# Delta rule of a two-model transformer kernel: the chunk inverse on four 64x64 tiles, with its transpose accumulated on the other half of the partitions

## The reference

```python
    decay = jnp.exp(jnp.where(causal, gcum[..., :, None] - gcum[..., None, :], -jnp.inf))
    kb = kc * bc[..., None]
    m = jnp.where(strict, jnp.einsum('nbhid,nbhjd->nbhij', kb, kc) * decay, 0.0)
    eye = jnp.eye(CHUNK, dtype=f32)
    t_inv = lax.linalg.triangular_solve(eye + m, jnp.broadcast_to(eye, m.shape), left_side=True, lower=True)
    u = t_inv @ (vc * bc[..., None])
    w = t_inv @ (kb * jnp.exp(gcum)[..., None])
    qk = jnp.einsum('nbhid,nbhjd->nbhij', qc, kc) * decay
```

## Time and profile before

| | us |
|---|---|
| median of three runs | 2900.84 |
| the profiled execution, its own time | 2904.52 |
| its span in the profile | 2902.7 |
| TensorE busy, matmuls | 2799.6 (96%) |
| VectorE busy | 2083.9 (72%) |
| ScalarE busy | 1454.1 (50%) |

### The profile page before, as it was taken

How to read it: one execution, slowest core, us unless ns; L and a number is a source line. 1 busy time by engine, 2 the same in 40 slices (tenths; PEclk the granted TensorE clock), 3 DMA queues, 4 the chain that set the end, 5 groups by cost and what they waited for, 6 DMA issues and landing times. The chain is left out here.

```text
span 2902.7 us, 53557 instructions
## 1 busy us (share of the span) xinstructions
PE 2799.6 (96%) x22724; PEld 2498.5 (86%) x22724; DVE 2083.9 (72%) x3259; ACT 1454.1 (50%) x1957; POOL 154.4 (5%) x257
## 2 busy tenths in 40 slices
PE   6999999999999999999999999999999999999998
PEld 6888899888888888998888878889788988887887
DVE  7986867668878868676786577755676677657774
ACT  3545644545445466446454355544554445435552
POOL 1000000200000000002000040000100000005000
PEclk7999999999999999999999999999999999999999
DMA  9775337538768753274475633555365556561552
GB/s 307 247 247 161 118 104 223 170 122 270 236 215 260 246 161 118 96 226 160 146 242 179 199 111 126 190 178 175 104 204 186 189 167 196 177 220 59 165 188 97
DMA packets 516702, 521.41 MB, mean 180 GB/s; under 512 B 16503, under 2 KB 513728, under 8 KB 516464
## 3 DMA queue, kind: packets, MB, share of 16 engines
q1 hardware_dynamic: 513856, 517.28, 55.5%
q0 software_dynamic: 816, 0.27, 0.1%
q10 hardware_dynamic: 1792, 0.44, 0.1%
HBM read 516.90 MB, written 1.05 MB: 178 GB/s over the span
## 5 line engine op out<-in xcount | busy, mean ns | idle before, releaser
L65 PE MATMUL P<-HX,wsp 128*128 128x256 f32 (+1 forms) x10304 | 1601.0, 317 | 24.5 <-DVE HX L82 16.9
L65 PEld LDWEIGHTS P<-HX,wsp 128*128 128x128 f32 x10304 | 1443.8, 191 | 161.3 <-issue 27.3
L74 DVE TENSOR_TENSOR wsp<-raw,wsp 128x2048 fp32r<-128x2048 f32 (+4 forms) x440 | 945.6, 2152 | 335.0 <-ACT wsp L71 334.4
L71 ACT ACTIVATE wsp<-raw 128x2048 fp32r<-128x2048 f32 (+4 forms) x440 | 790.9, 1799 | 533.4 <-PE P L65 454.6
L65 PE MATMUL P<-FG,wsp 128*128 128x256 f32 (+1 forms) x2816 | 495.4, 337 | 0.0
L65 PEld LDWEIGHTS P<-FG,wsp 128*128 128x128 f32 x2816 | 428.5, 188 | 62.5 <-DVE wsp L74 0.3
L71 ACT ACTIVATE arena<-P 128x512 f32<-128x512 f32 (+3 forms) x384 | 214.6, 567 | 510.1 <-PE P L65 506.3
L74 DVE TENSOR_TENSOR arena<-arena,P 128x512 f32<-128x512 f32 (+2 forms) x232 | 150.9, 652 | 176.9 <-ACT arena L71 148.0
L82 DVE SCALAR_TENSOR_TENSOR ACC<-raw,sm,ACC 128x256 f32<-128x256 f32 x476 | 230.8, 485 | 16.7
L65 PE MATMUL P<-arena 64*64 64x64 f32 (+9 forms) x4000 | 225.8, 260 | 13.7 <-ACT arena L71 8.9
L65 PE MATMUL P<-GX,wsp 128*128 128x256 f32 (+1 forms) x1592 | 227.9, 303 | 0.8 <-DVE GX L74 0.8
(11 more groups left out here) (110 smaller groups left out, 1382.8 us busy)
## 6 DMA issues: line engine op xcount, KB each, us to landing
raw<-in_ffn_w SPq DMA_DIRECT2D x120, 1024.0 KB, 5.3
raw<-in_ada_w SPq DMA_DIRECT2D x72, 1024.0 KB, 5.0
raw<-in_w_in SPq DMA_DIRECT2D x52, 1024.0 KB, 5.1
raw<-in_ffn_w_gate SPq DMA_DIRECT2D x44, 1024.0 KB, 5.3
raw<-in_ffn_w_up SPq DMA_DIRECT2D x44, 1024.0 KB, 5.3
raw<-in_ffn_w_down SPq DMA_DIRECT2D x32, 1024.0 KB, 5.1
raw<-in_nsa_w_in SPq DMA_DIRECT2D x20, 1024.0 KB, 8.0
raw<-in_ffn_w SPq DMA_DIRECT2D x16, 768.0 KB, 4.5
```

Source lines behind the costliest of these rows:

```text
L65: return self if self.e is None else self.e.matmul(*a, skip_group_check=True, **k)
L71: return self if self.e is None else self.e.activation(*a, **k)
L74: return self if self.e is None else self.e.tensor_tensor(*a)
```

## The change

`first`, `products` and `update` replace the inverse's loops on TensorE. The four chunks go as two groups `t` of two chunks (eight matrices a head), with one bank for the inverse (`u`) and one for its transpose (`t`) of each group. The products `x` land on the other half of the partitions, so that the update of the inverse uses the two quarters of the array off the diagonal and that of its transpose the two on it, and the four follow one another in the order of issue. Level 0 has no product: VectorE masks M with level 0 and adds an identity, and TensorE writes that and its transpose (`first`). Copies by ScalarE are 128x2x256, first both of `u`, then both of `t`; the mask on VectorE is one 128x512 instruction a group.

GpSimd does all factors of M ahead of the masks of the queries. The convolution's last taps and SiLU (piece 11), and the exponentials `eb`, move from before the inverse into its levels 1 and 2; `kt` moves to levels 2 to 5 and `vt` to levels 3 to 5. `plan_ada` puts two pieces of `ada_w` instead of four ahead of the last z piece, and two instead of one behind the branch pieces 0 and 2.

```diff
-            plan_ada(4, "steps")
+            plan_ada(2, "steps")
             cols(("z", l), wi, w256, 3840)
             for c in range(4):
                 cols(("ga", l), wi, w256, 4816 + 256 * c)
                 cols(("wa", l), A["w_branch_a"][l], w256, 256 * c)
-                plan_ada(1)
+                plan_ada(2 if c % 2 == 0 else 1)
@@ delta_pe
+            def first(t):
+                u, v = take(e, (l, "u", t)), take(e, (l, "t", t))
+                e.wait_ge(*DVC.at((l, "t1", t)))
+                for x in range(8):
+                    for q in range(2):
+                        i64, w = ident[half(q), half(q)], T1ST[t][half(q), x, :]
+                        o = 256 * (x // 4) + 64 * (x % 4)
+                        e.matmul(P[u][half(q), o:o + 64], w, i64, start=x == 0, stop=False)
+                        ins = e.matmul(P[v][half(1 - q), o:o + 64], i64, w, start=x == 0, stop=False)
+                ins.then_inc(*DMM.up((l, "ut", 0, t)))
+            def products(s, t):
+                b = take(e, (l, "x", s, t))
+                e.wait_ge(*DAC.at((l, "u", s - 1, t)))
...
+                        ins = e.matmul(P[b][half(1 - q), 64 * x:64 * x + 64], MKQ[c][half(q), 0, hp, :], UT[c][half(q), 0, hp, :], start=True, stop=True)
+            def update(s, t):
...
+                e.wait_ge(*DVC.at((l, "x", s, t)))
+                e.wait_ge(*DAC.at((l, "t", s - 1, t)))
...
+                    for q in range(2):
+                        T, W = UT[c][half(1 - q), 1, hp, :], XX[t][half(1 - q), x, :]
+                        ins = e.matmul(P[u][half(q), o:o + 64], T, W, start=False, stop=s == 5)
+                        if s < 5:
+                            ins = e.matmul(P[v][half(1 - q), o:o + 64], W, T, start=False, stop=s == 4)
+            first(0)
+            first(1)
+            for s in range(1, 6):
+                products(s, 0)
+                products(s, 1)
+                if s < 3:
+                    eb(s - 1)
+                if s >= 2:
+                    turned("kt", s - 2)
+                if s == 3:
                     e.wait_ge(*SIL.at((l, 11)))
+                if s >= 3:
+                    turned("vt", s - 3)
+                if s == 5:
+                    turned("vt", 3)
+                update(s, 0)
+                update(s, 1)
@@ delta_act
+            for s in range(6):
+                if s in (1, 2):
...
+                        e.activation(EB[c].rearrange("p h j -> p (h j)"), P[bank[l, "eb", c]][:, :], ACT.Exp).then_inc(*DAC.up((l, "eb", c)))
+                if s == 5:
+                    values(2)
+                for a in range(2 if s < 5 else 1):
+                    for t in range(2):
...
+                if s == 2:
+                    conv_silu_act(e, l, 11)
+                if s >= 3:
+                    values((0, 1, 3)[s - 3])
```

More of the change, by code:

```diff
@@ L1336, in delta_ada, with delta_steps @@
         def delta_ada(l):
-            return [nada[U["z", l][2] + 1 + i] for i in range(4)]
+            return [nada[U["z", l][2] + 1 + i] for i in range(2)]
+        def delta_steps(l):
+            return [(j, q) for j in delta_ada(l) for q in range(8)]
         def sums_dve(e, l):
@@ L1363, in delta_pe, with eb @@
                 give((l, "qk", c), DVC.at((l, "m", c)), DVC.at((l, "qd", c)))
-            for t in range(2):
+            def eb(t):
                 bs = [take(e, (l, "eb", 2 * t + r)) for r in range(2)]
@@ new lines, in turned @@
+                give((l, name, c), DVC.at((l, "kd" if c < 3 else "kt", c)) if name == "kt" else DAC.at((l, "v", c)))
+            def first(t):
[8 more added lines that the diff above has]
+                ins.then_inc(*DMM.up((l, "ut", 0, t)))
@@ new lines, in products @@
+            def products(s, t):
+                b = take(e, (l, "x", s, t))
+                e.wait_ge(*DAC.at((l, "u", s - 1, t)))
+                for x in range(8):
+                    c, hp = 2 * t + x // 4, x % 4
+                    for q in range(2):
+                        ins = e.matmul(P[b][half(1 - q), 64 * x:64 * x + 64], MKQ[c][half(q), 0, hp, :], UT[c][half(q), 0, hp, :], start=True, stop=True)
+                ins.then_inc(*DMM.up((l, "x", s, t)))
+                give((l, "x", s, t), DVC.at((l, "x", s, t)))
@@ new lines, in update @@
+            def update(s, t):
+                u, v = bank[l, "u", t], bank[l, "t", t]
+                e.wait_ge(*DVC.at((l, "x", s, t)))
+                e.wait_ge(*DAC.at((l, "t", s - 1, t)))
+                for x in range(8):
+                    c, hp = 2 * t + x // 4, x % 4
+                    o = 256 * (x // 4) + 64 * hp
+                    for q in range(2):
+                        T, W = UT[c][half(1 - q), 1, hp, :], XX[t][half(1 - q), x, :]
+                        ins = e.matmul(P[u][half(q), o:o + 64], T, W, start=False, stop=s == 5)
+                        if s < 5:
+                            ins = e.matmul(P[v][half(1 - q), o:o + 64], W, T, start=False, stop=s == 4)
+                ins.then_inc(*DMM.up((l, "ut", s, t)))
+                if s == 4:
+                    give((l, "t", t), DAC.at((l, "t", 4, t)))
+                if s == 5:
+                    give((l, "u", t), DAC.at((l, "u", 5, t)))
@@ L1506, in delta_pe @@
             outs(0)
-            ada_pe(e, delta_ada(l)[2])
+            ada_pe(e, delta_ada(l)[0])
             ws(1)
@@ L1513, in delta_pe @@
             kv(2)
-            ada_pe(e, delta_ada(l)[3])
+            ada_pe(e, delta_ada(l)[1])
             outs(2)
@@ L1522, in delta_act @@
                 e.activation(MKQ[c].rearrange("p a h j -> p (a h j)"), P[bank[l, "dd", c]][:, :], ACT.Exp).then_inc(*DAC.up((l, "dd", c)))
[L1523 to L1538 removed]
+            conv_silu_act(e, l, 10)
@@ L1589, in delta_dve @@
                         e.tensor_tensor(qe, qe, eb, ALU.mult).then_inc(*DVC.up((l, "qe", c)))
-                if s == 1:
-                    ready_dve(e, U["qkv", l][11])
-                n = (5, 1, 5, 5, 3, 3)[s]
-                for j, q in steps[first:first + n]:
+                n = (0, 0, 4, 2, 2)[s - 1]
+                for j, q in steps[done:done + n]:
                     ada_step(e, j, q)
-                first += n
-            for j, q in steps[22:24]:
-                ada_step(e, j, q)
+                done += n
+            ready_dve(e, U["qkv", l][11])
             def state(c):
@@ L1637, in delta_pool @@
                 e.tensor_tensor(MKQ[c][:, 0], MKQ[c][:, 0], pair_cols(BB, c).broadcast_to([128, 4, 64]), ALU.mult).then_inc(*DPL.up((l, "m", c)))
+            for c in range(4):
                 e.tensor_tensor(MKQ[c][:, 1], MKQ[c][:, 1], LE.unsqueeze(1).broadcast_to([128, 4, 64]), ALU.mult).then_inc(*DPL.up((l, "q", c)))
```

147 lines of the change are left out of this document (61 added, 86 removed).

## The result

| | median, us | range | runs |
|---|---|---|---|
| before | 2902.11 | 2899.47 to 2910.89 | 20 |
| after | 2898.91 | 2893.94 to 2902.40 | 20 |

The ratio is 0.9988, 95% interval 0.9982 to 0.9993: the change gains 3.5 us (2.0 to 5.2), where 17 were forecast and the range began at 4.8. The forecast was wrong. The two traces differ by 9.7 us of span and flatter the change.

What follows compares the result with a forecast made beforehand. TensorE, busy 96% of the span, was taken to bound the kernel through its quantity of matmuls. Inverse -12.6 and -10.4, branch stalls +3.0 and +3.0: -17.0 us, from the median 2900.84 to 2884; range 2872 to 2896.

Steps and rivals of the forecast that it cites:

- Inverse: Delta rule's inverse, level 0 and levels 1 to 5 together: 12.6 us gained in layer 1, 10.4 in layer 2.
- The start: Level 0, where `first` waits for VectorE: level 1 starts 9.8 us earlier in layer 1, 9.7 in layer 2.
- The levels: Levels 1 to 5 of the inverse: 29.7 us a layer, against 32.45 and 30.44 before.
- the waits for ScalarE: TensorE idle in the levels: 1.5 us for the SiLU in level 3, 0.75 each in levels 4 and 5.
- "issue": TensorE idle in the levels for supply of instructions: taken as 1.5 us a layer, bounded by 0 and 9.3.
- "instructions" as a rival: Rival: instruction supply or VectorE sets the pace of the levels, giving 2894 to 2900 us; chance 15%.
- a clock below 1.00 in the levels: Sign named beforehand as showing the forecast wrong: TensorE's clock below 1.00 in the inverse's levels.
- the tail keeps its 18.9 us: Tail behind the inverse's levels: length unchanged at 18.9 us.
- Branch: Next gate piece waits for VectorE's low half behind two `ada_w` pieces: TensorE stalls 3.0 us in each layer.
- The rival on the clock: Rival, also "slower: the clock": added waits halve the clock through the inverse, 27 us more a layer, 2938 us; chance 3%.
- no stall at the branch: Rival: VectorE starts the two `ada_w` pieces earlier, so the gate piece does not wait; 2878 us; chance 10%.
- four quarters don't help: Rival: row halves writing one bank take turns, updates and `first` stay at 29 ns; 2902 us, no change; chance 7%.

Runs made afterwards that it cites:

- after_again: The changed kernel run again with nothing edited, for a second profile and median: 2900.54 us, 0.9995 of the kernel before.
- before_again: The kernel before run once more with nothing edited, for a second profile: one run, 2899.53 us.
- loads_held: Changed kernel with second `ada_w` pieces behind branch pieces 2 and 3, and SyncE's next two weight loads held until the tail's last output matmuls: 2888.69 us, 0.9945 of before.

## Why the prediction was wrong

Means over the four profiled layers of after and after_again, against the four of before and before_again:

- **Inverse: -23.0 forecast, -20.7 measured** (38.0 for 48.35 a layer). The start was missized, 8.0 us on average for 7.1: mask and addition were priced at 1.4 us and took 2.1 beside GpSimd. The price came from rows in a stretch where GpSimd was busy for 1.58 of 45.71 us, and of an instruction that reads PSUM. The levels were forecast at 29.7 and took 30.8, 28.6, 30.3 and 30.1, 29.9 on average, but by luck in part. TensorE was busy in them for 26.6 to 27.0 us where the clock was full, against 25.2 in the forecast; the waits for ScalarE were 1.2 to 1.5 us instead of 3.0 (SiLU 1.18 for 1.5, and of the two `vt` waits of 0.75 none shows in layer 1 and one of 0.27 in layer 2); and "issue" was 2.2 us in layer 1 and 0.6 and 1.7 in layer 2, for 1.5 in both. So the array's rate was right; "instructions" as a rival was real at a quarter of its full price of 9.3 us at most. The forecast named a clock below 1.00 in the levels as a sign of being wrong, and it came in one of these four layers (0.97).
- **Tail: 0 forecast, +1.6 measured** (19.55 for 18.75 a layer). The step that failed is "the tail keeps its 18.9 us". I priced the moved loads as cost 0, since their data is needed 50 us later. They arrive two at a time in the tail and hold up the packets of instructions that TensorE lives on: shown by loads_held and by the 7.4 us between two packets.
- **Branch: +6.0 forecast, +7.0 for the longer stage (3.5 a layer), and +3.1 for half clock behind it.** The waits themselves are as forecast, 1.20 + 1.80 = 3.0 us a layer; the other 0.5 a layer goes with the second piece's sums, 0.40 us of `C,ACC` records, which the forecast set off against the inverse. The half clock is the other step that failed: I let a stall cost its length. The rival on the clock had it in the wrong place and size: it was to hold half clock through an inverse. What came are single stretches of 3.4 or 6.8 us, each costing 1 to 2.5.
- **z pieces: 0 forecast, +1.5 measured** (33.9 for 33.2). Half clock behind the sums came in 13 of 22 layers with the new inverse and 1 of 6 with the old. Whether the change makes this likelier or chance did, stays open.

These sum to -20.7 + 1.6 + 7.0 + 3.1 + 1.5 = -7.5 us. The spans of two and two profiles differ by -5.0. Of the 2.4 us between, 0.5 stand at the later branch pieces, where the other moved sums of `ada_w` are, and 1.9 in parts that no kernel edits (0.4 ahead of the first `qk`, 1.1 between the layers, 0.4 behind layer 2), which scatter by 5 us from profile to profile. The medians say -3.5, and -1.5 for after_again.

Of the chances: "no stall at the branch" was excluded, "four quarters don't help" fell (15.0 ns a record), "slower: the clock" was real but small. The range failed with them: all its terms took a clock of 1.00, a branch stall of at most its length, and a tail that nothing touches.

## What to carry to other kernels

A wait on a saturated TensorE costs more than its length, as the clock may halve behind it: look for another slot for the work that causes it before counting the gain of what it made room for. Here the slot was two pieces later, one line of a plan, worth 10 to 12 us. When matmuls get faster by running on more quarters, count instructions, not only busy time, and keep weight loads away from where they run dense. And profile the same kernel twice before explaining a difference of a few us.

## What the runs showed of the hardware

- Four-quarter 64x64 matmuls start every 15.0 ns (two-quarter ones 29.9), with both row halves writing one bank. The Trainium skill, "TensorE: Matmul & The Clock Gate", Wait — 56ns, not 53.3ns?, has starts at least 25 ns apart, and in "TensorEngine Tiling (Array Packing)", Restrictions and Gotchas, has no two row tiles in one bank at a time. Neither limit shows here.
- TensorE's instructions come in 16 KB packets, one for some 127 matmul records with their weight loads (22564 records and 178 packets of after, 2.92 MB):

```profile
q8 instruction: 178, 2.92, 0.4%
```

- The shortest time between two packets in all sixteen profiles was 3.23 us, that is 25 ns a matmul; at 15 ns a record 127 are used in 1.9 us. All 79 idles of over 0.3 us that only "issue" ends, between first `qk` and first z piece, ended 1.2 to 1.6 us after a packet had landed. That dense stretches first run on what was fetched ahead is argued from this.
- Two 1 MB weight loads side by side (DMA share 1.07 in the window) delayed TensorE by 1.2 us without any matmul needing their data: two packets of instructions stood 7.4 us apart around them, and at most 5.0 apart with the loads held.
- Half clock, mostly for 3.4 or 6.8 us on end, came at every stall at the branch, in 11 of 16 layers at the two waits of 1 us that `first` has, and in some executions and not in others behind 2 us of one-column matmuls in which the engine counted as busy all along.
